# A weight tile stored as even and odd columns, and read back by TensorE from its two halves in turn

## The reference, cut to what matters

```python
h = h + fox_mixer(rms_norm(h, mix_norm), fox_w_in, ..., fox_w_out)            # 2048 -> 3 x 2048 (+16), 2048 -> 2048
h = h + conv_ffn(rms_norm(h, ffn_norm), w_up, conv_w, conv_b, w_down)          # 2048 -> 2 x 5632, 5632 -> 2048
h = h + mixer_block(rms_norm_2(h, norm_mix_w_2), w_in_2, ..., w_branch_a_2, w_branch_b_2, w_out_2)
h = h + jnp.square(jax.nn.relu(rms_norm_2(h, norm_mlp_w_2) @ w_up_2)) @ w_down_2   # 2048 -> 8192 -> 2048
return rms_norm_2(h, norm_final_w_2)
```

## Time and profile before

| | before |
|---|---|
| median of three runs | 2549.34 us (2549.13 to 2549.86) |
| profiled execution: own time | 2552.38 us |
| its span, first to last instruction | 2550.6 us |
| TensorE busy (matmuls) | 2527.9 us, 99% |
| weight loads busy | 2100.0 us, 82% |
| VectorE busy | 1642.0 us, 64% |
| ScalarE busy | 1281.3 us, 50% |
| GpSimd busy | 214.3 us, 8% |
| DMA | 545.79 MB, mean 214 GB/s |

### The profile page before, as it was taken

How to read it: one execution, slowest core, us unless ns; L and a number is a source line. 1 busy time by engine, 2 the same in 40 slices (tenths; PEclk the granted TensorE clock), 3 DMA queues, 4 the chain that set the end, 5 groups by cost and what they waited for, 6 DMA issues and landing times. The chain is left out here.

```text
span 2550.6 us, 32506 instructions
## 1 busy us (share of the span) xinstructions
PE 2527.9 (99%) x11468; PEld 2100.0 (82%) x11468; DVE 1642.0 (64%) x1831; ACT 1281.3 (50%) x1617; POOL 214.3 (8%) x365
## 2 busy tenths in 40 slices
PE   8999999999999999999999999999999999999998
PEld 7888888888888888888888888888888888888886
DVE  5666665776666666776776655466566656666665
ACT  5555555655555555554344545454544444444444
POOL 0111101100000000000010100000110000000000
PEclk9999999999999999999999999999999999999999
DMA  7777777877777777767565766577776777777775
GB/s 233 258 202 220 208 213 221 240 223 226 225 224 227 222 227 221 212 182 217 177 192 174 238 189 190 173 213 246 235 223 206 230 208 220 214 223 212 215 220 156
DMA packets 270391, 545.79 MB, mean 214 GB/s; under 512 B 22011, under 2 KB 23395, under 8 KB 270179
## 3 DMA queue, kind: packets, MB, share of 16 engines
q1 hardware_dynamic: 244064, 469.82, 61.5%
q0 software_dynamic: 22192, 70.28, 9.9%
q10 hardware_dynamic: 4051, 4.59, 0.5%
HBM read 508.93 MB, written 35.68 MB: 214 GB/s over the span
## 5 line engine op out<-in xcount | busy, mean ns | idle before, releaser
L1391 DVE TENSOR_TENSOR w_lo<-raw,w_hi 128x1024 fp32r<-128x1024 f32 x887 | 1079.5, 1221 | 772.3 <-ACT w_hi L880 769.0
L880 ACT ACTIVATE w_hi<-raw 128x1024 fp32r<-128x1024 f32 x887 | 938.2, 1059 | 1039.5 <-PE acc L482 957.7
L480 PE MATMUL acc<-w_hi,A_hi 128*128 128x512 f32 x1932 | 762.1, 394 | 0.7 <-DVE w_lo L1391 0.5
L481 PE MATMUL acc<-w_lo,A_hi 128*128 128x512 f32 x1932 | 752.4, 389 | 0.0
L482 PE MATMUL acc<-w_hi,A_lo 128*128 128x512 f32 x1932 | 752.4, 389 | 0.0
L482 PEld LDWEIGHTS acc<-w_hi,A_lo 128*128 128x128 f32 x1932 | 362.8, 188 | 76.2
L480 PEld LDWEIGHTS acc<-w_hi,A_hi 128*128 128x128 f32 x1932 | 362.9, 188 | 75.2 <-DVE w_lo L1391 0.7
L481 PEld LDWEIGHTS acc<-w_lo,A_hi 128*128 128x128 f32 x1932 | 363.0, 188 | 73.4
L480 PE MATMUL acc<-w_hi,B_hi 128*128 128x512 f32 x800 | 312.6, 391 | 0.0
L480 PE MATMUL acc<-w_hi,C_hi 128*128 128x512 f32 x800 | 311.4, 389 | 0.5 <-DVE resid L1438 0.5
L482 PE MATMUL acc<-w_hi,B_lo 128*128 128x512 f32 x800 | 311.3, 389 | 0.0
(11 more groups left out here) (208 smaller groups left out, 1298.0 us busy)
## 6 DMA issues: line engine op xcount, KB each, us to landing
raw<-in_up SPq DMA_DIRECT2D x304, 512.0 KB, 4.4
raw<-in_w SPq DMA_DIRECT2D x271, 512.0 KB, 4.3
raw<-in_down SPq DMA_DIRECT2D x216, 512.0 KB, 4.6
raw<-in_wo SPq DMA_DIRECT2D x64, 512.0 KB, 5.0
turn_rows<-scratch POOLq DMA_DIRECT2D x23, 512.0 KB, 3.2
scratch<-turn_rows POOLq DMA_DIRECT2D x92, 128.0 KB, 5.8
up_rows<-scratch POOLq DMA_DIRECT2D x21, 512.0 KB, 5.2
scratch<-up_rows POOLq DMA_DIRECT2D x84, 128.0 KB, 5.1
```

Source lines behind the costliest of these rows:

```text
L480: pe.matmul(o, hi[:, kt, ts], wh, start=first and kk == 0, stop=False)
L481: pe.matmul(o, hi[:, kt, ts], wl, start=False, stop=False)
L880: act.activation(w_hi[:, q % RING, :], raw[:, q % RING, :], ACT.Copy).then_inc(w_hi_ready, 1)
L1391: dve.tensor_tensor(w_lo[:, q % RING, :], raw[:, q % RING, :], f32(w_hi[:, q % RING, :]), ALU.subtract).then_inc(w_lo_ready, 1)
```

## The change

Each row block of 512 columns in `w_hi` and `w_lo` is now stored as its 256 even columns followed by its 256 odd ones. The splits read `raw` in order and write column 0 to the first half, column 1 to the second (256 float32, 1024 bytes, further on), column 2 to the first again. VectorE reads `w_hi` in that same alternating way. The matmuls read column 0 of the first half, column 0 of the second, column 1 of the first and so on, so that the columns stream in their old order, and write PSUM in order as before. Nothing else is touched: the same instructions on the same engines in the same order with the same semaphores, the same number of elements each.

```diff
+        def even_odd(v):
+            return v.rearrange("p (k n h) -> p k n h", n=CW // 2, h=2)
+        def by_half(v):
+            return v.rearrange("p (k h n) -> p k n h", n=CW // 2, h=2)
+        def in_turn(w):
+            return w.rearrange("p (h n) -> p n h", h=2)
+        def columns(o):
+            return o.rearrange("p (n h) -> p n h", h=2)
...
-                        wh, wl = (w[:, ring, kk * CW:(kk + 1) * CW] for w in (w_hi, w_lo))
-                        o, ts = acc[:, banks[t], :], slice(t * P, (t + 1) * P)
+                        wh, wl = (in_turn(w[:, ring, kk * CW:(kk + 1) * CW]) for w in (w_hi, w_lo))
+                        o, ts = columns(acc[:, banks[t], :]), slice(t * P, (t + 1) * P)
                         pe.matmul(o, hi[:, kt, ts], wh, start=first and kk == 0, stop=False)
                         pe.matmul(o, hi[:, kt, ts], wl, start=False, stop=False)
                         m = pe.matmul(o, lo[:, kt, ts], wh, start=False, stop=last and kk == SLOT_K - 1)
...
-                act.activation(w_hi[:, q % RING, :], raw[:, q % RING, :], ACT.Copy).then_inc(w_hi_ready, 1)
+                act.activation(by_half(w_hi[:, q % RING, :]), even_odd(raw[:, q % RING, :]), ACT.Copy).then_inc(w_hi_ready, 1)
...
-                dve.tensor_tensor(w_lo[:, q % RING, :], raw[:, q % RING, :], f32(w_hi[:, q % RING, :]),
-                                  ALU.subtract).then_inc(w_lo_ready, 1)
+                dve.tensor_tensor(by_half(w_lo[:, q % RING, :]), even_odd(raw[:, q % RING, :]),
+                                  f32(by_half(w_hi[:, q % RING, :])), ALU.subtract).then_inc(w_lo_ready, 1)
```

More of the change, by code:

```diff
@@ L521, in gemm_first @@
                     pe.wait_ge((w0_hi, w_hi_ready)[kk], 1)
-                    wh, wl = (w[:, 0, kk * CW:(kk + 1) * CW] for w in (w_hi, w_lo))
+                    wh, wl = (in_turn(w[:, 0, kk * CW:(kk + 1) * CW]) for w in (w_hi, w_lo))
+                    o = [columns(acc[:, b, :]) for b in BK[0]]
                     for t in range(TT):
-                        pe.matmul(acc[:, BK[0][t], :], A_hi[:, kk, t * P:(t + 1) * P], wh, start=kk == 0, stop=False)
+                        pe.matmul(o[t], A_hi[:, kk, t * P:(t + 1) * P], wh, start=kk == 0, stop=False)
                     pe.wait_ge((w0_lo, w_lo_ready)[kk], 1)
                     for t in range(TT):
-                        pe.matmul(acc[:, BK[0][t], :], A_hi[:, kk, t * P:(t + 1) * P], wl, start=False, stop=False)
+                        pe.matmul(o[t], A_hi[:, kk, t * P:(t + 1) * P], wl, start=False, stop=False)
                     pe.wait_ge(early_lo, kk + 1)
                     for t in range(TT):
-                        m = pe.matmul(acc[:, BK[0][t], :], A_lo[:, kk, t * P:(t + 1) * P], wh, start=False, stop=False)
+                        m = pe.matmul(o[t], A_lo[:, kk, t * P:(t + 1) * P], wh, start=False, stop=False)
                     if kk == 0:
@@ L856, in last_downs @@
                             pe.wait_ge(w_lo_ready, RING * (R_END - 2) + q + 1)
-                        o, ts = acc[:, D2_LAST[q // 2][t], :], slice(t * P, (t + 1) * P)
+                        o, ts = columns(acc[:, D2_LAST[q // 2][t], :]), slice(t * P, (t + 1) * P)
                         for kk in range(SLOT_K):
-                            wh, wl = (w[:, q % RING, kk * CW:(kk + 1) * CW] for w in (w_hi, w_lo))
+                            wh, wl = (in_turn(w[:, q % RING, kk * CW:(kk + 1) * CW]) for w in (w_hi, w_lo))
                             kt, last = q % 2 * SLOT_K + kk, q % 2 == 1 and kk == SLOT_K - 1
@@ L958, in early_split @@
                 v = slice(kk * CW, (kk + 1) * CW)
-                return act.activation(w_hi[:, 0, v], raw[:, 0, v], ACT.Copy)
+                return act.activation(by_half(w_hi[:, 0, v]), even_odd(raw[:, 0, v]), ACT.Copy)
             act.wait_ge(w_early, 16)
@@ L1473, in early_split @@
                 dve.wait_ge((w0_hi, w_hi_ready)[kk], 1)
-                return dve.tensor_tensor(w_lo[:, 0, v], raw[:, 0, v], f32(w_hi[:, 0, v]), ALU.subtract)
+                return dve.tensor_tensor(by_half(w_lo[:, 0, v]), even_odd(raw[:, 0, v]), f32(by_half(w_hi[:, 0, v])), ALU.subtract)
             early_split(0).then_inc(w0_lo, 1)
```

## The result

| | before | after |
|---|---|---|
| median | 2549.6 us (4 runs) | 2752.88 us (2746.77 to 2758.47, 4 runs) |
| ratio | | 1.0795, 95% interval 1.0767 to 1.0823 |
| span of the profiled execution | 2550.6 us | 2747.1 us |

The page of the changed kernel: busy times, then the groups that answer to the earlier trace rows (line 1391 is now 1408, 880 is 897, 480 is 496).

What follows compares the result with a forecast made beforehand. TensorE was taken as the bound, by matmul count times start distance. From the profiled 2552.4 us, 119 less for matmuls, nothing for splits and 3 more for side effects gave 2436.4, hence a median of 2434 us; range 2403 to 2690.

Steps and rivals of the forecast that it cites:

- What bounds the kernel: TensorE: time is number of matmuls by distance between starts, 0.2267 us, a sixteenth lost in the moving operand's read.
- rival B: TensorE's moving read: no change, 2549 us, the lost sixteenth being a limit on columns under way, not addresses; chance 0.13.
- Step 1: Moving operand of the large matmuls on TensorE: distance falls from 226.7 to 215.5 ns, 119 us less.
- step 4: What a faster TensorE triggers: denser loads, some waits for loads showing, VectorE busier; 3 us added.
- Step 2: Splits on ScalarE and VectorE with alternating access: nothing added; upper bounds about 1.9 and 2.29 us, hidden by slack.
- rows 10: Profile rows of `make_level` with stepped access, used to price the splits: the pattern costs at most 13 ns of 684.
- rival C: TensorE's moving read halves: every large matmul at 427 ns, about 4680 us; chance 0.18.
- Rival A: VectorE's split becomes the bound at a second cycle an element, 949 us more busy time, 2630 us; chance 0.20.

Runs made afterwards that it cites:

- G = 2: Against the changed kernel: pairs of columns, not single ones, go in turn to slot halves 2048 bytes apart, matmuls reading them back; 3698.5 us, ratio 1.4501.
- step 2: Against the changed kernel: columns of the two halves stored woven, matmuls reading every other float32 in two passes; 4933.2 us, ratio 1.9346.
- grains of 16, 4 and 2: Against the changed kernel: groups of 16, 4 or 2 columns from slot halves 2048 bytes apart in turn; 2685.7, 2792.8 and 3698.5 us.

## Why the prediction was wrong, step by step

- *What bounds the kernel* held. TensorE's distance of 226.7 ns was a limit of the moving read, and another order lifts it; that rules rival B out.
- *Step 1, the matmuls.* 215.5 ns forecast, 215.9 measured; 119 us less forecast. The matmuls alone give 2550.4 - 2444.8 = 106 us: TensorE's busy time fell by 114.6 us, and of the difference some is new waits (idle 22.7 to 29.3), for which step 4 had 3 us. Step 4 also read ScalarE's waits for loads from two of five tensors; all five that the view lists are 76 us in 38 places, not 49.1 in 25.
- *Step 2, the splits, is the step that failed:* "I take nothing for the splits". The nearest row was `make_level` with a step of 2 floats. There two elements still fall on 16 bytes; in the change none do. The experiments put the cost where that row cannot see it: writes with 16 bytes to themselves cost 0.8 to 1.1 us a split on either engine; with two to a line (G = 2) 84 ns on ScalarE and 5 on VectorE. (These runs don't part two readings of it, a lone write on its 16 bytes and a jump of 1024 bytes on every write: no kernel wrote with a step of 4 float32.) I had written beside rows 10 that at least two elements fall in each 16 bytes there, and chose the value of that row all the same.
- *The Trainium skill's rule.* "Advanced Engine Details and Errata", section "SBUF Cachelines", asks for two hits on a line. For the writes of ScalarE and VectorE the runs agree (2193 and 2192 ns with one, 1143 and 1226 with two at G = 2, 1129 and 1226 with a step of 2). For their reads they agree only in part (1311 and 1272 with one hit, and 1566 and 1507 with two where TensorE reads in turn). For TensorE's moving read they contradict it: one hit a line is the fastest order, 216 ns, and two hits in a row with a step of 2 the slowest, 451. The prediction took it as one rule for both and let it speak for rival C as much as for A.
- *Rival A* was the right mechanism for the right half of the change, with two wrong sizes. It priced VectorE's split at 2.29 us (2.19 measured) and its time at 2630 with VectorE alone; VectorE's write alone measures 2.02 us and 2556 us. And it left ScalarE out, whose split I had bounded at 1.9 us, a figure for which I showed no row (2.06 alone, 2.19 with both), and set aside because 5.2 us of slack cover a slow split. They cover one. With both slow, the loads wait for VectorE, ScalarE for the loads (78.2 us for `in_down` alone, against 8.9 before; for all five tensors 249 us against 76), VectorE for ScalarE, and TensorE's clock falls in the gaps: 2753, 63 us above the end of the range.
- The changed kernel against the matmuls alone, from the two profiles: 304.5 us of span, of it 205.6 more idle time of TensorE, up to 39 by the lower clock (0.983 of 2747 against 0.997 of 2443), and about 60 in TensorE's busy time beside it. An estimate from the records accounts for them: the changed kernel's TensorE is idle before 238 matmuls instead of 11; after such a gap the next start follows 0.32 us later instead of 0.216, and the last matmul before it counts with its whole length, 0.38 us, instead of the distance 0.216. 227 x (0.104 + 0.164) = 61 us.
- *Rivals B and C* didn't happen here. An order of C's size exists (step 2, 451 ns), and the chance of 0.18 stood on the right doubt, the wrong pattern.

```profile
ACT w_hi L897 <- DMA raw<-in_down: 78.2, 65, 4.3
ACT w_hi L897 <- DMA raw<-in_up: 71.6, 62, 4.7
```

These two, of the changed kernel, answer to the earlier trace rows: waits for loads in 65 and 62 places where `in_up` had 16.

## What to carry to other kernels

When a consumer is the bound and wants another layout, price the producer's write pattern from a row with the same number of elements on each 16 bytes, not merely from one with "a step"; where no such row exists, the rival with the doubled producer deserves the first place. For a relayout from two places, try the irregular side on the reads: alternating over 1024 bytes, a split took 1311 and 1272 ns with its reads and 2.0 us or more with its writes, and the same stored layout cost 2193 and 2192 ns a split with writes in turn and 1566 and 1507 with stepped reads, which turned 8% slower into 2.6% faster. It is the pattern and not the side alone that counts: writes with a step of 2 took 1129 and 1226 ns, beside slower matmuls. Slack that covers one slow link of a chain says nothing of two.

## What the runs showed of the hardware that I had not expected

- TensorE's float32r moving read: 216 ns for 512 columns in turn from two runs 1024 or 2048 bytes apart, 227 in order, 233 backwards, 283 from four runs, 240, 254 and 334 with grains of 16, 4 and 2, 451 with step 2. Two runs with step 2 inside each: 227. I found no simple rule in these runs that gives all of them; this stays open.
- ScalarE's and VectorE's splits are 9 and 7% longer beside each other when both write in turn; when only one does, the other's split in order stays at 1.225 us (VectorE) or 1.058 us (ScalarE).
- A split that reads with a step of 2 depends on what TensorE reads meanwhile: 1.17 us on ScalarE and 1.23 on VectorE with no large matmul starting beside it, 1.60 and 1.53 us with seven that read in turn. Splits in order (1055 and 1222 ns) don't feel those matmuls.
- A float32r matmul read in order between two that read in turn starts its successor 232 ns later, 5 ns more than among its like.
